# Attention of a hybrid decoder step: by query tile with all heads' keys on chip, several heads per score slot, outputs as rows

## The reference

```python
def blk(start):
    qb = lax.dynamic_slice_in_dim(qp, start, Q_BLOCK, axis=1)
    s = jnp.einsum('bqhd,bkhd->bhqk', qb, kp).astype(jnp.float32) * ATTN_SCALE
    qpos = start + jnp.arange(Q_BLOCK)
    s = jnp.where(kpos[None, :] <= qpos[:, None], s, -jnp.inf)
    p = jax.nn.softmax(s, axis=-1)
    return jnp.einsum('bhqk,bkhd->bqhd', p.astype(vp.dtype), vp)
```

## Time and profile before

| | us |
|---|---|
| median of 3 runs | 2229.43 (2228.91 to 2236.23) |
| the profiled execution | 2228.98 |
| its span, first to last instruction | 2227.2 |
| mean granted clock of TensorE, share of 2.4 GHz | 0.952 |
| busy: TensorE / VectorE / ScalarE / GpSimd | 2040.1 / 1194.1 / 641.0 / 635.7 |

### The profile page before, as it was taken

The page is one execution under the profiler, slowest core; times in us unless marked ns, Lnnn a source line. Parts: engine busy times, 40 slices in busy tenths (PEclk is TensorE's granted clock), DMA queues, the critical chain, the costliest instruction groups (busy, mean ns, idle before and its releaser), DMA issues. The chain is left out here.

```text
span 2227.2 us, 35805 instructions
## 1 busy us (share of the span) xinstructions
PE 2040.1 (92%) x12589; PEld 1622.2 (73%) x12589; DVE 1194.1 (54%) x2166; ACT 641.0 (29%) x1347; POOL 635.7 (29%) x584
## 2 busy tenths in 40 slices
PE   8999999758888899999999939989999999999999
PEld 4566766435555677777777717879999999999997
DVE  4676676735545375556555644544544444444444
ACT  1323233223333344444444422121211111111110
POOL 1333434410000453233223323242323223232311
PEclk9999999768888799999999969989999999999999
DMA  5011111054130102222322133021101211111101
GB/s 213 21 36 41 36 55 38 27 134 114 45 97 0 41 20 54 69 60 78 87 60 71 44 99 121 29 76 57 39 19 57 57 57 40 30 43 57 57 19 76
DMA packets 174103, 131.93 MB, mean 59 GB/s; under 512 B 59725, under 2 KB 159422, under 8 KB 173862
## 3 DMA queue, kind: packets, MB, share of 16 engines
q1 hardware_dynamic: 170614, 129.37, 20.1%
q0 software_dynamic: 144, 1.08, 0.2%
q10 hardware_dynamic: 3232, 0.01, 0.1%
HBM read 110.81 MB, written 19.65 MB: 59 GB/s over the span
## 5 line engine op out<-in xcount | busy, mean ns | idle before, releaser
L2371 PE MATMUL f_ps<-nT_hi,f_gu_hi 128*128 128x344 f32 x1056 | 338.6, 321 | 6.7 <-POOL f_gu_lo L2243 6.7
L2371 PE MATMUL f_ps<-nT_hi,f_gu_lo 128*128 128x344 f32 x1056 | 338.0, 320 | 0.0
L2371 PE MATMUL f_ps<-nT_lo,f_gu_hi 128*128 128x344 f32 x1056 | 337.7, 320 | 0.0
L1479 POOL TENSOR_TENSOR s_b_latT<-s_b_latT_hi,s_b_latT_lo 128x1024 f32<-128x1024 f32 x64 | 155.2, 2425 | 343.1 <-DVE s_b_latT_lo L1533 343.0
L1600 DVE TENSOR_REDUCE s_b_ssq<-s_b_ksq 128x8 f32<-128x512 f32 x256 | 172.6, 684 | 120.2 <-ACT s_b_ksq L1397 118.2
L1397 ACT ACTIVATE s_b_ksq<-s_ps 128x512 f32<-128x512 f32 x256 | 153.1, 598 | 211.1 <-PE s_ps L1751 171.2
L1751 PE MATMUL s_ps<-s_b_wk_hi,s_b_latT_hi 128*128 128x512 f32 x512 | 206.8, 404 | 5.0 <-ACT s_b_ksq L1397 4.7
L2371 PEld LDWEIGHTS f_ps<-nT_hi,f_gu_hi 128*128 128x128 f32 x1056 | 199.4, 189 | 7.5 <-POOL f_gu_lo L2243 7.1
L1751 PE MATMUL s_ps<-s_b_wk_hi,s_b_latT_lo 128*128 128x512 f32 x512 | 200.4, 391 | 0.0
L1751 PE MATMUL s_ps<-s_b_wk_lo,s_b_latT_hi 128*128 128x512 f32 x512 | 200.1, 391 | 0.0
L2371 PEld LDWEIGHTS f_ps<-nT_lo,f_gu_hi 128*128 128x128 f32 x1056 | 198.9, 188 | 0.4
(11 more groups left out here) (357 smaller groups left out, 3640.5 us busy)
## 6 DMA issues: line engine op xcount, KB each, us to landing
p_latn<-in_cache_kv_latent SPq DMA_DIRECT2D x256, 128.0 KB, 2.0
gu_raw<-in_w_gate SPq DMA_DIRECT2D x22, 512.0 KB, 4.1
gu_raw<-in_w_up SPq DMA_DIRECT2D x22, 512.0 KB, 5.2
f_wd_raw<-in_w_down SPq DMA_DIRECT2D x11, 1024.0 KB, 5.0
t_w_in<-in_w_in SPq DMA_DIRECT2D x8, 980.0 KB, 13.3
t_x<-in_x_prompt SPq DMA_DIRECT2D x8, 512.0 KB, 5.5
p_krn<-in_cache_k_rope SPq DMA_DIRECT2D x256, 16.0 KB, 1.8
h<-in_w_out SPq DMA_DIRECT2D x8, 512.0 KB, 8.7
```

Source lines behind the costliest of these rows:

```text
L1479: out(pool.tensor_tensor(out=flat(latT), in0=flat(latT_hi).bitcast(F32), in1=flat(latT_lo).bitcast(F32), op=ALU.add), "sum_done")
L2371: ins = pe.matmul(ps[:, bank + j, 0:W], w[fi][:, j, k, :], x[:, k, cols], start=(k == 0 and w is gu_hi and x is nT_hi), stop=(k == KD - 1 ...
```

## The change

Attention is no longer done by pairs of heads. Queries, keys and values of all heads are loaded tile by tile of 128 positions, now counted from position 0, so that the meta tokens are part of the first block and every block has 128 rows. The work is a list of 45 units: for tile 0 one unit with eight heads, for tile 1 two with four heads, for tiles 2 and 3 four with two heads each, for tiles 4 to 7 eight with one head each; and for the 16 last queries two tails, each with four heads stacked in the partitions in groups of 32 rows. A unit's scores take three banks, and units alternate between two sets of three. For step n TensorE issues `turn(n-2)`, `scores(n)`, `values(n-2)`. The turned probabilities (128 columns) are now the stationary side and v (64 columns) moves, so outputs come as rows, query by query; copy and transpose back are gone, and VectorE's `finish` divides all heads of a tile in one instruction. VectorE copies the first half of the turned blocks (bank 6), ScalarE the second (bank 7). The mask is added by VectorE for all heads of a unit at once. There is no loop. SP queues all loads, then the pages of both first samples, then the stores by tile and eight small ones for the tails.

In the samples block semaphores that came in twos are merged into one with twice the count (`ha_done` and `hb_done` into `h_done`, and so on).

```diff
-        groups.append([blocks[b:b + 2] for b in range(0, len(blocks), 2)])
+    units = []
+    for t in range(NT):
+        nh = {0: 8, 1: 4, 2: 2, 3: 2}.get(t, 1)
+        units += [(t, list(range(h, h + nh))) for h in range(0, H, nh)]
+    for u, at in enumerate((39, 43)):
+        units.insert(at, (NT, list(range(u * HT, (u + 1) * HT))))
...
+        for t in range(NT + 1):
+            cols = slice(t * P, min(T, (t + 1) * P))
+            n = cols.stop - cols.start
+            sp.dma_start(k[:, :, cols], s["kT"][:, :, cols].rearrange("h d t -> d h t")).then_inc(loaded[load_of[t]], 16)
+            sp.dma_start(q[:, :, cols], s["qT"][:, :, cols].rearrange("h d t -> d h t")).then_inc(loaded[load_of[t]], 16)
+            sp.dma_start(v[0:n, t, :], s["v"][cols, :]).then_inc(loaded[load_of[t]], 16)
...
+                dve_steps(dve, dve.tensor_tensor(out=own, in0=own, in1=bc(mask[:, :], nh, 1), op=ALU.add))
...
+            dve_steps(dve, dve.tensor_reduce(m[:, 0:nh], src, AXX, ALU.max))
+            dve.tensor_scalar(nmx[n % 4][:, 0:nh], m[:, 0:nh], -SCALE, None, ALU.mult).then_inc(max_ready, 1)
...
-                    ins = pe.matmul(ps[h * VD:(h + 1) * VD, o_bank(n), 0:R], v[par][0:w, blk, h * VD:(h + 1) * VD],
-                                    pt[gg % 2][0:w, b, h, 0:R], start=(blk == 0), stop=(blk == groups[n][-1][-1]))
...
+                        ins = pe.matmul(ps[:, o_bank(t), h * VD:(h + 1) * VD], pt[g][:, c, :], v[:, b, h * VD:(h + 1) * VD],
+                                        start=(b == 0), stop=(b == t))
...
+                        ins = pe.matmul(ps[j * QT:(j + 1) * QT, TAIL_BANK, VD:2 * VD], src[0:w, j * QT:(j + 1) * QT],
+                                        v[0:w, b, h * VD:(h + 1) * VD], start=(b == 0), stop=(b == NT))
...
-        with pe.Fori(0, PAIRS // 2) as i:
-            pair(i, 0)
-            pair(i, 1)
+        for n in range(K + 2):
+            if n >= 2:
+                turn(n - 2)
+            if n < K:
+                scores(n)
+            if n >= 2:
+                values(n - 2)
```

More of the change, by code:

```diff
@@ L973, in attention_block @@
     ctx = ExitStack()
-    sb = lambda name, shape: ctx.enter_context(nc.sbuf_tensor("a_" + name, shape, F32))
+    sb = lambda name, shape, dt=F32: ctx.enter_context(nc.sbuf_tensor("a_" + name, shape, dt))
     sem = lambda name: ctx.enter_context(nc.semaphore("a_" + name))
[L976 to L983, removed]
-        groups.append([blocks[b:b + 2] for b in range(0, len(blocks), 2)])
@@ L985, in attention_block @@
-    first_group = [sum(len(g) for g in groups[:n]) for n in range(N + 1)]
-    G = first_group[N]
+    HT = 4
+    QT = 32
+    units = []
[4 more added lines that the diff above has]
+        units.insert(at, (NT, list(range(u * HT, (u + 1) * HT))))
+    K = len(units)
+    first_unit = [min(n for n in range(K) if units[n][0] == t) for t in range(NT)]
+    last_unit = [max(n for n in range(K) if units[n][0] == t) for t in range(NT)]
@@ L988, in attention_block @@
+    tails = [n for n in range(K) if units[n][0] == NT]
+    assert all(n % 2 == 1 for n in tails)
+    done_order = sorted([(last_unit[t], t) for t in range(NT)] + [(n, NT) for n in tails])
     ps = ctx.enter_context(nc.psum_tensor("a_ps", [P, 8, 512], F32))
     flat = ps[:, :, :].rearrange("p b c -> p (b c)")
[L990 to L993, removed]
@@ L1010, in attention_block, with o_bank, places, blocks_of @@
     block = ctx.enter_context(nc.Block())
[L1012 to L1017, removed]
+    def o_bank(t):
+        return 2 if t % 2 else 5
+    TAIL_BANK = 5
+    def places(n):
+        t, heads = units[n]
+        W = (t + 1) * P
+        per = max(1, 512 // W)
+        return [1536 * (n % 2) + (i // per) * 512 + (i % per) * W for i in range(len(heads))], W
+    def blocks_of(n):
+        t, heads = units[n]
+        blocks = [(i, h, b) for i, h in enumerate(heads) for b in range(t + 1)]
+        half = (len(blocks) + 1) // 2
+        return blocks[:half], blocks[half:]
@@ L1019, in _, with outputs, first_turns, is_tail @@
+    def outputs(n):
+        return [m for m, _ in done_order].index(n) + 1
+    def first_turns(n):
+        return n + 1 + sum(m < n for m in tails)
+    def is_tail(n):
+        return units[n][0] == NT
+    def output_done(n):
+        return is_tail(n) or n == last_unit[units[n][0]]
     @block.sync
     def _(sp):
[L1021 to L1046, removed]
@@ new lines, in _ @@
+        pages.load_ids_and_weights(sp)
+        pages.load(sp, 0, 0)
+        pages.load(sp, 1, 1)
+        for t in range(NT):
+            lo = META if t == 0 else 0
+            sp.wait_ge(att_done, outputs(last_unit[t]))
+            sp.dma_start(s["att"][t * P + lo - META:(t + 1) * P - META, :], att[lo:P, t, :]).then_inc(att_stored, 16)
+        for u in range(H // HT):
+            sp.wait_ge(att_done, outputs(tails[u]))
+            for j in range(HT):
+                h = u * HT + j
+                sp.dma_start(s["att"][SEQ - META:SEQ, h * VD:(h + 1) * VD],
+                             atail[j * QT + QT - META:(j + 1) * QT, u, :]).then_inc(att_stored, 16)
@@ L1084, in attention_block @@
-    EARLY, LATE = range(0, 2), range(2, NT)
+        pool_steps(pool, pool.memset(tmask[:, :], 0.0))
+        for j in range(HT):
+            own = slice(j * QT, (j + 1) * QT)
+            ins = pool.affine_select(out=tmask[own, :], in_=tmask[own, :], compare_op=ALU.is_ge, fill=NEG,
+                                     base=META - QT, pattern=[[-1, META]], channel_multiplier=1)
+        ins.then_inc(consts, 1)
     @block.vector
     def _(dve):
[L1088 to L1124, removed]
@@ L1126, in _ @@
+        dve.wait_ge(consts, 2)
+        for n in range(K + 3):
+            if 2 <= n < K + 2:
+                copy_first(n - 2)
+            if n < K:
+                maximum(n)
+            if n - 2 in tails:
+                copy_last(n - 2)
+            if n >= 3 and output_done(n - 3):
+                finish(n - 3)
     @block.scalar
     def _(act):
[L1128 to L1140, removed]
-                    if n >= 1:
-                        copy_groups(act, i, par, n - 1, 1, pt_copied[1], LATE)
-                        R = order[n - 1][1]
-                        act.wait_ge(o_ready, u * N + n)
-                        act.activation(oT[(n - 1) % 2][:, 0:R], ps[:, o_bank(n - 1), 0:R], ACT.Copy).then_inc(oT_copied, 1)
@@ new lines, in exps @@
+        def exps(n):
+            act.wait_ge(max_ready, n + 1)
+            if not is_tail(n):
+                t, heads = units[n]
+                at, W = places(n)
+                for i, h in enumerate(heads):
+                    ins = act.activation(prob[n % 2][:, i * W:(i + 1) * W], flat[:, at[i]:at[i] + W], ACT.Exp,
+                                         bias=nmx[n % 4][:, i:i + 1], scale=SCALE, accum_out=lsum[t][:, h:h + 1])
+            else:
+                u, lo = tails.index(n), 1536 * (n % 2)
+                ins = act.activation(prob[n % 2][:, :], flat[:, lo:lo + T], ACT.Exp, bias=nmx[n % 4][:, 0:1], scale=SCALE,
+                                     accum_out=ltail[:, u:u + 1])
+            ins.then_inc(exp_done, 1)
@@ new lines, in turn @@
+        def turn(n):
+            pe.wait_ge(exp_done, n + 1)
+            for g in range(2):
+                if n >= 1:
+                    pe.wait_ge(copied[g], first_turns(n) - 1 if g == 0 else n)
+                if not is_tail(n):
+                    t = units[n][0]
+                    cols = [(i * (t + 1) + b) * P for i, h, b in blocks_of(n)[g]]
+                else:
+                    cols = [(g * 4 + b) * P for b in range(4)]
+                for c, lo in enumerate(cols):
+                    ins = pe.transpose(ps[:, 6 + g, c * P:(c + 1) * P], prob[n % 2][:, lo:lo + P], ident[:, :])
+                ins.then_inc(turned[g], 1)
@@ L1530, in low_parts @@
             gg = group_of(b, g)
[L1531 to L1532 removed]
+            for bank in range(2):
+                dve.wait_ge(S["h_done"], 2 * gg + bank + 1)
                 out(dve.tensor_tensor(out=latT_lo[g % 2][:, :, 2 * bank:2 * bank + 2, :],
@@ L1696, in turn @@
             page = lambda j, lo, hi: latn[p][:, GP * g + j, lo:hi]
-            for bank, name in ((0, "a"), (1, "b")):
-                after(pe, f"l{name}_done", gg)
+            for bank in range(2):
+                after(pe, "l_done", 2 * gg + bank - 1)
                 for c in range(2):
```

230 lines of the change are left out of this document (125 added, 105 removed).

## The result

The changed kernel takes 2162.36 us (median of 4 runs, 2161.26 to 2165.03) against 2230.64 us of the kernel before in the same session: ratio 0.9691, 95% interval 0.9671 to 0.9712, 68 us less. The forecast was 2167 us. The profiled execution took 2163.0 us, with a span of 2161.3.

A forecast was written before the change was run, and what follows sets the result against it. It took attention to be bound by a score-to-transpose chain on one bank set plus four cold starts. With 166 us of TensorE work and 8 of stalls, attention ends 62 us earlier: 2229 - 62 = 2167 us, range 2152 to 2182 (2150 to 2198 with rivals).

The forecast's parts named there:

- What bounds the kernel now: Attention, 261 us: a chain from scores to transpose with a single set of score banks, plus four cold starts at low clock.
- TensorE's work: Attention at 2.4 GHz: transposes 31.7, scores 62.5, values 62.4, tails 9, together 166 us.
- price of 0.13 for a pair: Old values form, two heads side by side in the array halves: 0.13 us per (head, block), 37 us for 288.
- Cover: Attention steps: whether one step of slack hides VectorE's and ScalarE's work behind TensorE's; mostly yes, except tile 0.
- 8 us over 45 steps: Attention: allowance for hand-overs that aren't hidden and for the tail's last copy.
- margin of 0.3 us at 640 keys: Tightest one-head unit: vector work of 3.0 us fits into TensorE's 3.3 us of other work.
- Start and end: Attention's ends: first scores at 475.7, high clock by 490, last products 1 us, then 7 us of stores instead of 3.6.
- Outside: Samples stage with merged semaphores: nothing, at most 3 us for index arithmetic; feed-forward and mixing stages: nothing.
- 1 (no slack): Attention steps: each second copy arrives late by 0.6 us on the mean, 27 us instead of 8, 2186 us; chance 0.17.
- 2 and 3 (the clock): Attention: clock stays at 0.84, 2198 us, chance 0.15; or the whole stage runs at 1.2 GHz, 2328 us, chance 0.04.
- rival 2: Attention: 40% values, columns moving in half their weights' load time, keep the clock at 0.84; 31 us more, 2198; chance 0.15.
- 4: Attention: dearer values (25 us) and low clock in half the stage use up the gain, within 0.3%; chance 0.02.

The follow-up runs named there:

- no_slack: The changed kernel, but scores of unit n wait for the exponential of n-1 instead of n-2; 2205.67 us, ratio 0.9891.
- values_cols: The changed kernel with v stationary again and turned probabilities moving, outputs as columns not turned back (output not the reference's); 2147.24 us, ratio 0.9629.

## Why the prediction was right, point by point

**What bounds the kernel now.** Half right. The four cold starts were the larger part: changes of pair with 6.4 us of idle time each, and the low clock behind them, 32 us of which are gone. The chain behind a single set of banks shows only there and at the short last tiles (19.3 us of waits for exponentials in all); in the long tiles TensorE waited for copies (14.2 us), which the text didn't name. The 44 us of no_slack are what the changed kernel would lose, with its shorter steps, and not what the kernel before lost.

**TensorE's work.** The sum of 166 us is what the trace has (165 by the estimate above): 3.24 us for a unit of 768 keys is the sum of the three prices to a hundredth or two, and the tails run four side by side: the 24 score records of one take 1.90 us (639.08 to 640.98), where the sixteen with 512 columns would need 6.7 one after the other at the 0.42 of the earlier trace rows. The 0.217 us for a value product, taken from the tiles block, was right. Its price against the old form was taken as 25 us; values_cols measured 15: with the old form a unit of that run is also 0.14 us longer than its parts, where half-array and full-array products follow each other, which the price of 0.13 for a pair left out.

**Cover.** "8 us over 45 steps" is the term that was mis-sized: 1.5 us were measured, 0.9 of it the tail's last copy. The margin of 0.3 us at 640 keys was enough: no step of that kind shows a wait.

**Start and end.** 7 us to the first scores became 6.4; the high clock by 490 came at 491.8 in one execution and at 499.8 in another (in the kernel before at 493.7, by 0.57 on the mean from 492 to 494 and 1.00 from there). End: 1 + 7 us forecast, 6.5 measured: a small store was issued in 0.46 us and not in 0.57, and the block ended 1.4 us behind the last issue, where it took 3.2 behind the full store of before. The block was forecast at 198 us and is 188.9.

**Outside.** "Nothing, at most 3 us" is the step that failed. The tiles block is 2.3 us longer, by no cause that is known, and the samples block 5.1. Each merged wait is for the same event, as the text said, but the merge adds instructions, one wait is 2.2 us longer wherever it is in, and alone it made the kernel before 9.6 us slower. That the arithmetic of the counts causes this is my reading. The 10 us too many inside the block and 6 too few outside left 4 to 5 in the total: that the forecast came so near is in part luck.

**Rivals.** 1 (no slack) fell: 1.5 us of waits instead of 27. 2 and 3 (the clock) fell: 0.99 from 490 on, and 1.00 even without most of the scores. What rival 2 says of the values is in the trace after: twelve value records have their weight loads one behind the other, 0.116 us apart from 562.15 to 563.54, where 64 columns would need 0.054 at the pace of the scores (four records, 1536 columns, in 1.29 us). The clock stayed at 1.00 all the same. 4 fell with the total. The prediction names two ranges, 2152 to 2182 for its own case and 2150 to 2198 with the rivals; the time lies in both.

**Open.** The tiles block, whose code is the same, takes 468.2 to 471.4 us over the traces; I have no cause. What decides the gaps at the feed-forward loop's jumps is open too: the rule by remainders of 64 was refuted twice.

## What to carry to other kernels

Before changing a pipeline, list what its busiest engine waits for and where. Here the waits of the kernel before stood at the changes of pair and at copies, and nearly half of the gain in the block (32 of 70 us) was the clock that had fallen behind those gaps. When the steps then get shorter, count again what TensorE can do between its scores and the exponential they need: a second set of banks, so that scores wait for the exponential of two steps ago, is worth 44 us in the changed kernel. Its idle time gone, TensorE's time was a plain sum of record distances, to 1%. A run that takes a part out of the new kernel prices that part there; it doesn't split the gain over the old one. A refactoring of semaphores isn't free either, 9.6 us alone here: measure it alone, and measure the blocks that were not edited, for the feed-forward moved by up to 22 us.

## What was not expected of the hardware

- Eight small products more (32 instructions of TensorE) in the attention block went with a feed-forward, itself untouched, that is 16.7 us longer (787.7 against 771.0 us): two gaps of 0.8 to 2.0 us at each of four jumps back, and 3.4 to 6.8 us at a clock of 0.50 behind them.
- Where half-array and full-array products follow each other, a unit with two such changes is 0.14 us longer than its parts (values_cols: scores 1.38 us instead of 1.29, transposes 0.71 instead of 0.66).
- The listed wait understates what a broken pipeline costs: 0.74 us listed, 1.0 lost in each step, 0.16 of it since the last transpose's latency counts as busy.
